# Three RWKV-7 units in flight: the chain of one beside the inverse of the next, the projections in one dense stretch

## What is computed

```python
res = x
for layer in (0, 1):
    shift, scale, gate = split(silu(c) @ ada_w[layer] + ada_b[layer])
    h = rms_norm(res, pre_g) * (1 + scale) + shift
    if layer == 0:
        out = (concat(pooling mixer, HGRN2 recurrence) * silu(gate path)) @ ev_w_out
    else:                                     # RWKV-7, 16 heads of 64
        xm = h + (shifted(h) - h) * mu        # six mixes: r k v z, decay, a
        r, k, v, z = xm[:4] @ w_rkvz
        decay = exp(-0.6065 * sigmoid(w0 + tanh(xm[4] @ w1) @ w2))
        a = sigmoid(a0 + (xm[5] @ a1) @ a2)
        kk = normalise(k * k_k);  k = k * (1 + (a - 1) * k_a)
        for t:                                # state S: 64 x 64 for each head
            S = S * decay[t] + (S @ -kk[t]) (kk[t] * a[t])^T + v[t] k[t]^T
            y[t] = S @ r[t]
        y = (y - mean(y)) * rsqrt(var(y) + eps) * lnx_g + lnx_b
        y = y + sum(r * k * r_k) * v
        out = (y * silu(z)) @ rw_w_out
    res = res + gate * rms_norm(out, post_g)
```

## Time and profile before

| | us |
|---|---|
| median of 3 runs | 4105.95 (4094.34 to 4109.58) |
| the profiled execution | 4104.3 |
| its span, first to last instruction | 4102.5 |
| mean granted clock of TensorE | 0.939 |
| PE busy | 3701.6 (90%) |
| PEld (weight loads, beside PE) busy | 2067.6 (50%) |
| DVE busy | 1727.1 (42%) |
| ACT busy | 1293.2 (32%) |
| POOL busy | 159.7 (4%) |

### The profile page before, as it was taken

The page is one execution under the profiler, slowest core; times in us unless marked ns, Lnnn a source line. Parts: engine busy times, 40 slices in busy tenths (PEclk is TensorE's granted clock), DMA queues, the critical chain, the costliest instruction groups (busy, mean ns, idle before and its releaser), DMA issues.

```text
span 4102.5 us, 72232 instructions
## 1 busy us (share of the span) xinstructions
PE 3701.6 (90%) x31690; PEld 2067.6 (50%) x31690; DVE 1727.1 (42%) x3702; ACT 1293.2 (32%) x2468; POOL 159.7 (4%) x183
## 2 busy tenths in 40 slices
PE   2997899999898899999989879999989987999998
PEld 1564445456455445555545535545445553545454
DVE  7254634343244544343325554334333446334342
ACT  1333333232233333233224333333223333333232
POOL 0000100000000100000000010000000001000000
PEclk9999899999999899999999989999999998999999
DMA  7211211011212211010131221011112212011011
GB/s 310 66 55 63 72 35 31 28 38 43 83 52 94 62 38 33 28 33 28 42 96 41 92 68 44 23 34 32 33 52 83 63 62 88 24 33 33 28 36 43
DMA packets 269489, 230.18 MB, mean 56 GB/s; under 512 B 15548, under 2 KB 251256, under 8 KB 266104
## 3 DMA queue, kind: packets, MB, share of 16 engines
q1 hardware_dynamic: 266872, 217.18, 16.5%
q0 software_dynamic: 2304, 8.39, 0.6%
HBM read 208.76 MB, written 16.78 MB: 55 GB/s over the span
## 4 chain that ended last, share of the span: by engine, by line
PE 76%; DVE 13%; ACT 7%; issue 2%; DMA 1%; SPq 0%; DVEq 0%; ACTq 0%
PE bank L529 16%; PE bank L395 12%; PE bank L488 7%; PE bank L599 5%; PE bank L471 5%; PE bank L625 4%; PE bank L623 3%; PE bank L428 3%; PE bank L392 3%; DVE xm L1257 3%; PE bank L519 2%; PE bank L668 2%; PE bank L663 2%; PE bank L651 2%; PE bank L581 2%
## 5 line engine op out<-in xcount | busy, mean ns | idle before, releaser
L529 PE MATMUL bank<-xm,wring 128*128 128x512 f32 x2048 | 1117.1, 650 | 69.4 <-ACT arena L908 35.4
L395 PE MATMUL bank<-arena,wring 128*128 128x512 f32 x1280 | 580.1, 593 | 14.0 <-ACT xm L754 10.2
L529 PEld LDWEIGHTS bank<-xm,wring 128*128 128x128 f32 x2048 | 347.5, 196 | 340.1 <-issue 190.3
L395 PEld LDWEIGHTS bank<-arena,wring 128*128 128x128 f32 x1280 | 230.7, 190 | 259.1 <-issue 254.5
L488 PE MATMUL bank<-wring,yT 128*128 128x512 f32 x608 | 280.1, 624 | 32.4 <-DVE yT L1290 22.3
L1348 DVE COPY_PREDICATED r_Q<-smask,bank 128x128 f32<-128x128 uint8 x320 | 104.1, 325 | 387.4 <-PE bank L599 387.4
L945 ACT ACTIVATE arena<-Mcur,arena 128x64 f32<-128x64 f32 x256 | 89.2, 348 | 548.1 <-DVE Mcur L1370 548.1
L471 PE MATMUL bank<-wring,yT 128*128 128x512 f32 x416 | 222.4, 641 | 0.0
L599 PE MATMUL bank<-arena 64*64 64x32 f32 x5120 | 212.3, 223 | 8.7 <-DVE arena L1348 7.5
L488 PEld LDWEIGHTS bank<-wring,yT 128*128 128x128 f32 x608 | 121.1, 200 | 191.4 <-issue 152.4
L625 PE MATMUL bank<-arena,r_Q 64*64 64x32 f32 x5120 | 210.7, 223 | 0.4 <-issue 0.4
(11 more groups left out here) (263 smaller groups left out, 5166.2 us busy)
## 6 DMA issues: line engine op xcount, KB each, us to landing
wring<-in_rw_w_rkvz SPq DMA_DIRECT2D x128, 512.0 KB, 4.0
wring<-in_ev_w_in SPq DMA_DIRECT2D x96, 512.0 KB, 5.1
xm<-in_ada_w SPq DMA_DIRECT2D x16, 1536.0 KB, 11.2
wring<-in_ev_w_out SPq DMA_DIRECT2D x32, 512.0 KB, 8.2
wring<-in_rw_w_out SPq DMA_DIRECT2D x32, 512.0 KB, 3.5
xm<-in_x POOLq DMA_DIRECT2D x16, 512.0 KB, 6.6
arena<-in_x SPq DMA_DIRECT2D x16, 512.0 KB, 6.0
residual_scratch<-arena SPq DMA_DIRECT2D x4, 2048.0 KB, 7.5
```

The costliest lines, as they stand in the source:

```text
L395: mm = pe.matmul(pj[:, :], w[:, k, :], hT[:, k, 1:1 + TB], start=(k == 0), stop=(k == KC - 1))
L529: mm = pe.matmul(pj[:, :], w[:, k, :], xmv[MIX_OF[i - 2]][:, k, :], start=(k == 0), stop=(k == KC - 1))
```

## The change

The order within a unit is laid out anew, in periods. Period p (from -1 to 7) has unit p in its chain, unit p+1 in its inverse and unit p+2 in its projections:

- First a dense stretch on PE: the values and keys of p are turned, V of p+1, the variance of p-1, the bonus sum and the scores of p+1, the rest of V, LoRA and K, key sum and R of p+2, and Z of p+1. No projection stands in the chain any more.
- Then a stretch of 64x64 tiles only: the eight chunks of unit p, in whose three gaps stand the 30 parts of the inverse of unit p+1 (`QUARTER_INV` says how many in each gap, six gaps to a row). Period -1 has an inverse and no chain, period 7 a chain (beside the output projection) and no inverse.
- The chain's matmuls with 128 rows (values and u together) are split in two of 64 rows, so that those with the values can go ahead: 16 matmuls a chunk for 12. The state is kept in Mall; Mcur and its copies are gone.
- The values are centred as they are turned (multiplied by the identity less 1/64), so the mean's matmul and its subtraction are gone; y is copied and squared by ACT straight from the bank, and the finish has three operations for four.
- The inverse starts from the masked scores, which DVE copies into Y (`umask`), and not from products with the identity. r_Q has two levels for five, and POOL refills it after each level; POOL also fills Y.
- Banks 0, 1 and 4 are shared by turns (`BANK0`, `BANK1`, `BANKM`), two banks serve the inverse, and AR, Gs, Y, z, the bonus and the decays at the chunk ends exist twice. r_BK moves into yT. reset128 moves into the arena, so POOL fills it again at each block's start, once the units of the block before are finished; its prefetch of x stands behind that.

```diff
-RN = 2 + 4 * KC
-RN_CHAIN = 2 + 2 * KC + 2
 LV_INV = 5
-ARENA = 15136
+INV_PARTS = 6 * LV_INV
+ARENA = 17184
...
+QUARTER_INV = [[2, 1, 2, 1, 2, 0], [2, 1, 2, 1, 2, 0], [2, 1, 1, 1, 2, 0], [2, 1, 1, 1, 2, 0]]
+INV_CUT = [0]
+for _n in sum(QUARTER_INV, []):
+    INV_CUT.append(INV_CUT[-1] + _n)
+assert INV_CUT[-1] == INV_PARTS
...
+BANK0 = [(m, p) for p in range(RP) for m in "krv"]
+BANK1 = [x for p in range(RP) for x in ([("var", p - 3)] if p >= 3 else []) + [("w", p), ("a", p), ("ks", p)]
+         + ([("z", p - 1)] if p else [])] + [("var", RP - 3), ("z", RP - 1), ("var", RP - 2)]
+BANKM = [("rk", 0)] + [x for p in range(RP) for x in [("bk", p)] + ([("rk", p + 1)] if p + 1 < RP else [])] + [("var", RP - 1)]
...
+        IV = [bank[2], bank[3]]
+        SCORES = [bank[5], bank[6], bank[2], bank[3]]
...
+        cent64 = sb("cent64", [P, 64])
+        umask = sb("umask", [P, 32], U8)
+        r_Q = sb("r_Q", [P, 2, NCH * 64])
         lmask = sb("lmask", [P, 8, 128], U8)
...
+                def weights(p, m):
+                    s = 4 * (p % 2) + m
+                    load(s, use_rwkv(b, p // 2, s), rkvz_v[RKVZ[m], p:p + 1][0], slot_k(s))
+
+                for p in range(-2, RP):
+                    if 0 <= p + 1 < RP:
+                        weights(p + 1, PROJ_V)
+                    if p + 2 < RP:
+                        sp.wait_ge(S["w2_free"], 1 + b * RP + p + 2)
                         for i, n in enumerate(("rw_w2", "rw_a2")):
-                            sp.dma_start(w2a2[64 * i:64 * i + 64, q, :],
-                                         io[n][0, :, ds((2 * pp + q) * P, P)]).then_inc(S["w2_in"], 16)
+                            sp.dma_start(w2a2[64 * i:64 * i + 64, p % 2, :],
+                                         io[n][0, :, ds((p + 2) * P, P)]).then_inc(S["w2_in"], 16)
+                        weights(p + 2, PROJ_K)
+                        weights(p + 2, PROJ_R)
+                    if 0 <= p + 1 < RP:
+                        weights(p + 1, PROJ_Z)
...
+            def variance(b, p):
+                pe.wait_ge(S["y_sb"], b * RP + p + 1)
+                if p == RP - 1:
+                    pe.wait_ge(S["ms_free"], turn(BANKM, b, "var", p))
+                    pe.matmul(MS[:, :], blk[:, :], r_yd, start=True, stop=True).then_inc(S["ms_ready"], 1)
+                else:
+                    pe.wait_ge(S["b1_free"], turn(BANK1, b, "var", p))
+                    pe.matmul(bank[1][:, :], blk[:, :], r_yd, start=True, stop=True).then_inc(S["b1_ready"], 1)
...
+            def turn_values(b, p):
+
+                pe.wait_ge(S["b0_free"], turn(BANK0, b, "v", p) + 1)
                 for c in range(NCH):
+                        r = half_of(h)
+                        mm = pe.matmul(XB[r, c * RC:(c + 1) * RC], r_v[r, c * RC:(c + 1) * RC], cent64[r, :],
+                                       start=True, stop=True)
...
+                def keys_values(c):
+                    for h in range(2):
+                        r, g = half_of(h), gs_at(c, h)
+                        pe.matmul(XB[half_of(1 - h), 0:64], G[r, g:g + 64], r_VT[r, c * RC:(c + 1) * RC], start=True, stop=False)
...
+                    pe.wait_ge(S["ixy"], (v + 1) * 2 * LV_INV)
+                    pe.wait_ge(S["v_tok"], v + 1)
+                    pe.wait_ge(S["bkt"], v + 1)
+                    pe.wait_ge(S["ms_free"], turn(BANKM, b, "bk", p) + 1)
+                    pe.wait_ge(S["y_sb"], v)
+                    if p + 1 < RP:
+                        pe.wait_ge(S["sc_free"], (v + 1) * 4 + 2)
+                    keys_values(0)
+                pe.wait_ge(S["ch_m"], v * NCH + c)
+                for h, r, s, g in heads:
...
-                    pe.matmul(YB[r, c * RC:(c + 1) * RC], Mcur[r, :], r_AR[r, r_c], start=True, stop=False)
+                pe.wait_ge(S["y_ready"], v * NCH + c)
+                for h, r, s, g in heads:
+                    pe.matmul(YB[r, cc], M[r, :], AR[r, c * P + 64:(c + 1) * P], start=True, stop=False)
+                for h, r, s, g in heads:
+                    pe.matmul(UZ[r, 0:64], r_BKt[r, c * P + 64 * h:c * P + 64 * h + 64], r_VT[r, cc], start=True, stop=False)
                 ahead(0)
...
+            def period(b, p):
+
+                inv, pre = p + 1 < RP, p + 2 < RP
+                if p < 0:
+                    project(b, 0, PROJ_V, 0, KC)
+                    project(b, 1, PROJ_K, 0, KC)
+                    bonus_sum(b, 0)
+                    scores(b, 0)
+                else:
+                    turn_values(b, p)
+                    turn_keys(b, p, 0)
+                    if inv:
+                        project(b, p + 1, PROJ_V, 0, 3)
+                    turn_keys(b, p, 1)
+                    if inv:
+                        project(b, p + 1, PROJ_V, 3, 5)
+                    if p:
+                        variance(b, p - 1)
+                    if inv:
+                        bonus_sum(b, p + 1)
+                        project(b, p + 1, PROJ_V, 5, 6)
+                        scores(b, p + 1)
+                        project(b, p + 1, PROJ_V, 6, KC)
+                if not inv:
+                    pe.wait_ge(S["b0_free"], turn(BANK0, b, "v", p) + 1)
+                    pe.wait_ge(S["b1_free"], turn(BANK1, b, "var", p - 1) + 1)
+                if not inv:
+                    quarter(b, p, 0)
+                if pre:
+                    lora_up(b, p + 2, 0)
+                    if p >= 0:
+                        project(b, p + 2, PROJ_K, 0, KC)
+                    lora_up(b, p + 2, 1)
+                if pre:
+                    key_sum(b, p + 2)
+                    project(b, p + 2, PROJ_R, 0, KC)
+                if inv:
+                    project(b, p + 1, PROJ_Z, 0, KC)
+                    quarter(b, p, 0)
+                quarter(b, p, 1)
+                quarter(b, p, 2)
+                if not inv:
+                    pe.wait_ge(S["r_done"], 1 + b * RP + p)
+                quarter(b, p, 3)
...
+            def y_copy(b, p):
+                v = b * RP + p
+                act.wait_ge(S["y_ready"], (v + 1) * NCH)
+                act.wait_ge(S["r_done"], 1 + v)
+                act.copy(r_y, YB[:, :])
+                act.activation(r_yd, YB[:, :], ACT.Square).then_inc(S["y_sb"], 1)
...
+            def rwkv_masks(b, p):
+                v = b * RP + p
+                G, Y = r_Gs[p % 2], r_Y[p % 2]
...
+                    s = half_of(1 - h)
+                    y = Y[s, :].rearrange("p (a c x z) -> p a c x z", a=2, c=4, z=2)[:, :, :, :, 1]
+                    n = G[s, :].rearrange("p (a h c x z) -> p a h c x z", a=2, h=2, c=4, z=2)[:, :, h, :, 0:32, 1]
+                    for a in range(2):
+                        own(V.copy_predicated(y[:, a], umask[s, None, :].to_broadcast([64, 4, 32]), n[:, a]))
...
+            def rwkv_finish(b, p):
+                V.wait_ge(S["r_var"], b * RP + p + 1)
+                step(V.scalar_tensor_tensor(out=r_y, in0=r_y, scalar=par("lnx_g", p), in1=r_yd, op0=ALU.mult, op1=ALU.mult))
+                step(V.scalar_tensor_tensor(out=r_y, in0=r_y, scalar=par("lnx_b", p), in1=r_bv[p % 2], op0=ALU.add, op1=ALU.add))
+                V.tensor_tensor(yTv[:, p, :], r_y, r_z[p % 2], ALU.mult).then_inc(S["r_done"], 1)
...
+            def rwkv_period(b, p):
+                inv, pre = p + 1 < RP, p + 2 < RP
+                if inv:
+                    rwkv_operands(b, p + 1)
+                    rwkv_masks(b, p + 1)
+                if not inv:
+                    rwkv_quarter(b, p, 0)
+                if p >= 0:
+                    rwkv_gate(b, p)
+                if pre:
+                    rwkv_scan(b, p + 2)
+                if not inv:
+                    rwkv_quarter(b, p, 1)
+                    rwkv_quarter(b, p, 2)
+                if pre:
+                    rwkv_key(b, p + 2)
+                if pre:
+                    rwkv_rates(b, p + 2)
+                if p >= 1:
+                    rwkv_finish(b, p - 1)
+                if inv:
+                    rwkv_bonus(b, p + 1)
+                    rwkv_quarter(b, p, 0)
+                    rwkv_quarter(b, p, 1)
+                    rwkv_quarter(b, p, 2)
+                rwkv_quarter(b, p, 3)
+                own.restart()
...
+                if b:
+                    gp.wait_ge(S["r_done"], 1 + b * RP)
+                own(gp.memset(reset128, 1.0))
+                own.wait()
+                gp.memset(reset128.rearrange("p (c t) -> p c t", t=HC)[:, :, 0:1], 0.0).then_inc(S["h_rst"], 1)
+                gp.wait_ge(S["b0_free"], b * len(BANK0))
...
+                for v in range(b * RP, (b + 1) * RP):
+                    gp.wait_ge(S["iq_ready"], v * 12)
+                    gp.wait_ge(S["ixy"], v * 2 * LV_INV)
+                    if v > 1:
+                        gp.wait_ge(S["y_ready"], (v - 1) * NCH)
+                    for t in (r_X, r_Y[v % 2]):
```

(8 more changed lines are left out.)

746 lines of the change are left out of this document (371 added, 375 removed).

## The result

The changed kernel took 3798.89 us (median of four runs, 3780.53 to 3811.01) against 4103.01 for the kernel before in the same comparison (4094.34 to 4109.58): a ratio of 0.926, 95% interval 0.921 to 0.930. The sign was right and the size was not: 304 us less where 133 were forecast (the time lies inside the stated range, at its low end). The profiled execution took 3795.61 us, 308.7 less than the profiled one of before.

The account below looks back on a forecast made before the run. PE was taken as the bound. A steady unit of 62.8 + 5.9 = 68.7 us against 73.6, with the block ends, saved 33 us a block, 133 in four: 4104.3 - 133 = 3971 us; range 3783 to 4130.

Parts of the forecast that it names:

- The clock term: Steady period: clock drop 19 to 23 us into the small-tile stretch, costing 4.5 to 7.7 us; 5.9 charged.
- rival C: Small-tile stretch: clock drops 9 us into it, 78.4 us a unit, slower by 140: 4244 us; chance 0.10.
- rival A: Steady units: no clock drop costs anything, or it falls only at the end; 62.8 to 65 us, 3837 us; chance 0.20.
- The sum without any drop: Whole kernel by the skill's rule that the clock falls only after PE was idle: 3971 - 28 x 5.9 = 3806 us.
- The small-tile stretch: Inverse and chain in 64x64 tiles: 14.1 for 30 parts, 7.4 for the chain, 1.5 and 1.2 besides; 24.2 us.
- exposed round trips and POOL: Small-tile stretch: 1.5 us of uncovered DVE round trips in every second chunk's last gap, and 1.2 for POOL's copies.
- the dense stretch: Steady period's PE work before the small tiles, including 37 matmuls at 0.86 us and 1.2 us waiting: 38.6 us.
- the mean: Dense stretch: the mean's 512-column matmul is gone; norm behind the last chain 2.3 us shorter.
- the tile turns: Steady unit: each turn between 128x128 and 64x64 tiles costs PE some 0.2 us; about 4 us saved.
- period 6: Near a block's end, without K, R, LoRA and key sum: 20.3 + 24.2 + 5.9, 50.4 us.
- rival B: Side work of DVE, ACT or POOL is late, 3 to 4 us a unit: 4055 to 4097 us; chance 0.14.
- the opening of a block: Before period 0: 13.3 us more than the 74.4 before, and 3 more for the clock under the first inverse.

Follow-up runs that it names:

- the long run: Changed kernel with the eight matmuls of the inverse's first part done 22 times instead of once in chunk 0's first gap, periods 0 to 6: 4059.79 us (0.991).
- the 64-row matmuls: Changed kernel with four unread 64-row, 512-column matmuls added in the second gap of chunk 6, periods 0 to 6: 3897.02 us (0.949).
- four and five repeats: Changed kernel with DVE's bonus product in periods 0 to 5 repeated four or five additional times: 3820.34 us (0.931) and 3964.71 us (0.968).
- R's matmuls ahead: Changed kernel with the first two matmuls of projection R ahead of the key sum instead of behind it: 3749.23 us (0.916).

## Why the prediction was wrong in size

By the profiled executions the change saved 308.7 us, 175.7 more than the 133 of the sum. Periods 0 to 5 of the four blocks took 373.7, 364.8, 354.6 and 354.4 us, together 1447.5; the sum had 24 x 68.7 = 1648.8. That is 201 us, and it splits into two terms, 105 and 96.

**The clock term failed.** The step was: "The drop comes with the small tiles, while PE is busy 1.00, and it ends only after some microseconds of dense work", from which followed a drop 19 to 23 us into the stretch and 5.9 us a period. What the three drops in these 24 periods cost, with the waits ahead of them, is 1447.5 - 24 x 58.8 = 36 us, 1.5 a period where 5.9 were charged; 105 us of the miss. The reading of the rows was the fault. I looked at the microsecond in which the clock fell, where PE is busy 1.00, and took the tiles for the cause. A wait stood just ahead of it: 0.37 us, ending at 717.19, where the chain begins. The sum did not speak of it. The run with 30 us of small tiles shows that the length of the run alone does nothing; the kernel before with its waits filled shows that the waits did it. The drop 9 us into unit 7 of block 0, on which rival C was built, had another wait ahead of it, one with no releaser, while weights came in at 369 GB/s:

```profile
995.52 1.11 PE L599 MATMUL bank<-arena 64*64 64x32 f32 x30 [0.56 <-issue]
```

So rival A was the right one on the clock in steady periods, and its 3837 us the nearest of the rivals' numbers. It gives no reason why the clock would stay up, though, and leaves out the drops that are left.

The Trainium skill ("TensorE: Matmul & The Clock Gate", Why this matters for your kernels) puts a clock drop in the middle of a kernel down to an idle gap between bursts of matmuls. The prediction had set that aside because the trace seemed to disagree. The runs here agree that idle time comes first. They differ on how much it takes: the page warns only of gaps longer than any in the small-tile work of these two kernels, and here a wait of 0.37 us was followed by a drop in 26 units, and three waits of at most 0.22 us in each chunk in the run with the inverse in one piece. The sum without any drop was 3806 us, and that it lies so near 3799 is luck: it leaves out 82 us for the seven drops with their waits, and has some 110 us too much for the stretches at full clock.

**The small-tile stretch was mis-sized**: 20.7 us instead of 24.2, most of the other 96 us (24 x 4.0). The 2.7 us for exposed round trips and POOL came out as 0.9: the waits are three, of 0.27, 0.41 and 0.25 us, and no cost of POOL's copies shows in DVE's:

```profile
L1496 DVE SCALAR_TENSOR_TENSOR Mall<-bank,arena 128x64 f32<-128x64 f32 x256 | 71.6, 280 | 143.8 <-PE bank L700 143.8
L1492 DVE COPY arena<-bank 128x64 f32<-128x64 f32 x256 | 57.7, 225 | 144.2 <-PE bank L692 144.2
L1489 DVE COPY arena<-bank 128x64 f32<-128x64 f32 x256 | 57.5, 225 | 185.9 <-PE bank L682 183.6
```

225 and 280 ns are the means of before (224 and 284). The other 1.7 us is PE's own pace: 30 parts and the chain's 256 passes were summed to 21.5 us, and PE was busy 19.8. A part by itself took 0.467 us (9.8 us for 21 of them in the long run), as forecast, so if the parts keep that pace the chain's passes take (19.8 - 14.0) / 256 = 0.023 us beside them, not 0.029. The timeline has matmuls of the chain (L700) and of the inverse (L649) alternating:

```profile
798.83 0.22 PE L649 MATMUL bank<-arena,r_Q 64*64 64x32 f32 x1
798.83 0.22 PE L700 MATMUL bank<-arena 64*64 64x64 f32 x1
798.83 0.22 PE L649 MATMUL bank<-arena,r_Q 64*64 64x32 f32 x1
798.84 0.22 PE L700 MATMUL bank<-arena 64*64 64x64 f32 x1
```

That matmuls of the two streams run beside each other is read from these rows; no run tested it.

**Right:** the dense stretch (38.0 for 38.6), with the wait of the key sum at 1.12 us for the 1.2 forecast:

```profile
602.16 1.10 PE L566 MATMUL bank<-arena,blk 128*128 128x512 f32 x2 [1.12 <-ACT arena L952]
```

Right too were the mean, the tile turns, no wait before the scores in a steady period, period 6 (50.4 forecast, 50.3 to 54.4 measured, though that is luck, as the account is another: 40.9 without a wait, 1.5 of wait and 8 or 12 of clock, instead of 44.5 and 5.9 of clock), and the warning of rival B, which came true in period 6 alone.

**Against the change:** the opening of a block. The prediction's window of the earlier trace rows begins at 423.28, inside the first projection, which begins at 418.75:

```profile
418.75 5.46 PE L529 MATMUL bank<-xm,wring 128*128 128x512 f32 x6 [3.45 <-DVE xm L1257]
```

From there it was 78.9 us to the first chain, and the prediction's 13.3 and 3 make 95.2 to period 0; measured were 102.5 (417.41 to 519.95), 7.3 more. PE has a wait of 2.70 us at 450.87, where ACT's copies for the LoRA end, shorter ones (0.8 to 1.0 us) for ACT's sigmoids and copies, and a clock drop at 450 us that the kernel before did not have there. The later blocks open alike, so this is some 29 us in four; periods 6 and 7 took 9 us more in all than in the sum. That leaves 201 - 38 = 163 of the 176 us. The other 13 or so came outside these stretches: block 0's first projection begins 1.3 us earlier, and from the last chain of a block to the next block's first projection it is 2 to 5 us less than before. I did not follow them.

**Open:** why a wait of 0.37 us ahead of the chain brought a drop in nearly every unit of the kernel before, while the changed kernel's three waits, up to 0.41 us, brought none in the 21 periods that had no long wait. Not the length of the run and not the 64-row matmuls; what else differs was not tried. The length of a single wait doesn't settle it, as a drop also followed one of 0.19 us, and none followed some of 1.5 us. Nor was it tried whether a wait of 0.7 us in another place of the stretch would count more.

## What to carry to other kernels

When the clock falls inside small-tile work, look for PE's waits in the microseconds ahead of the fall, not at the busy share in it: here 1.5 us of waiting cost 8 to 12 more in clock where the clock fell, and five useless matmuls in each short wait paid for themselves. Interleaving two chains of small matmuls then gains twice, once by the overlap (10.2 us a period) and once by keeping PE fed. And when a stage loses its dense work at the end of a loop, ask which side work that had covered, and which loads now land beside the small tiles.

## What the hardware showed that I had not expected

- A wait that depends on the DMA load: 1.4 to 2.4 us in which PE waits for nothing that the profile shows, inside small-tile work, beside or just behind weights that came in at up to 414 to 426 GB/s. With the loads moved into dense stretches the waits were gone.
- Useless matmuls that save time: 4176 us became 4071 in one order, 4103 became 4027 in the other.
- The same wait with two outcomes: 1.47 us at the first link brought a drop in 19 of 20 periods of one run. The 1.52 us of period 6 brought one in all 16 periods of four kernels (the changed one, four and five repeats, the loads held back), in three of four in two more (R's matmuls ahead, the 64-row matmuls), and in only two of four with the mean put back; 0.74 us in 2 of 20. A sum for the clock has to be a chance times a price. What decides between the outcomes is open.
